# The diagonal of the other core's rows, masked through V instead of through the exponential

## The reference, cut to what matters

```python
s = einsum('bqhcd,bkhcd->bhcqk', qb, k) * scale          # two maps c per head h
s = where(dist >= 0, s - slope[h] * dist, -inf)          # causal, ALiBi
p = softmax(s)
a = p[:, :, 0] - lam * p[:, :, 1]
o = einsum('bhqk,bkhv->bqhv', a, v)                      # 4 heads, 128 value columns
```

## Time and profile before

| | us |
|---|---|
| median of 3 runs | 1221.82 (1221.73 to 1221.93) |
| the profiled execution, its own time | 1218.94 |
| its span on the slowest core (6) | 1217.4 |
| PE busy | 1154.6 (95%) |
| ACT busy | 652.8 (54%) |
| DVE busy | 601.8 (49%) |
| POOL busy | 80.7 (7%) |

### The profile page before, as it was taken

One profiled execution on the slowest core, in us unless ns is written; L12 is line 12 of the kernel. 1 busy time (PEld: TensorE's weight loads), 2 busy tenths in 40 slices (PEclk: granted clock), 3 DMA queues, 4 the chain that ended last, 5 costly groups with the idle time before them and its releaser, 6 DMA issues.

```text
span 1217.4 us, 27397 instructions; the slowest of 8 cores (1213.7 to 1217.4 us)
## 1 busy us (share of the span) xinstructions
PE 1154.6 (95%) x7340; PEld 578.0 (47%) x7464; DVE 601.8 (49%) x971; ACT 652.8 (54%) x1055; POOL 80.7 (7%) x139
## 2 busy tenths in 40 slices
PE   3799999999999999999999999999999999999995
PEld 1455444555555555554444444444444444444443
DVE  2666436553444333333365337336455463727767
ACT  4555358889898998976746773330211112030065
POOL 0000012111110000010000000000000000000012
PEclk9999999999999999999999999999999999999998
DMA  8487320002000000049441408011230403030124
GB/s 174 157 192 190 65 36 2 2 3 37 3 2 3 2 2 2 3 65 199 119 104 27 114 3 140 15 35 24 47 53 17 70 1 70 1 70 10 27 87 191
DMA packets 16903, 71.90 MB, mean 59 GB/s; under 512 B 2128, under 2 KB 2384, under 8 KB 14320
## 3 DMA queue, kind: packets, MB, share of 16 engines
q0 software_dynamic: 6768, 35.65, 17.9%
q1 hardware_dynamic: 9840, 33.97, 8.1%
q10 hardware_dynamic: 144, 0.52, 0.1%
HBM read 97.40 MB, written 8.39 MB: 87 GB/s over the span
## 4 chain that ended last, share of the span: by engine, by line
PE 88%; DMA 3%; DVE 3%; issue 3%; ACT 2%; DVEq 0%; SPq 0%; ACTq 0%; POOL 0%; POOLq 0%
PE ps_all L290 68%; PE ps_all L287 11%; PE ps_all L292 7%; DMA big<-w_g 2%; PE ps_all L311 2%; ACT big L582 1%; DVE big L314 1%; DMA big<-xs 1%; ACT big L298 0%; DVE big L1102 0%; DVE big L1120 0%; PE ps_all L657 0%; DVE big L625 0%; DVE big L974 0%; DVE big L1090 0%
## 5 line engine op out<-in xcount | busy, mean ns | idle before, releaser
L290 PE MATMUL ps_all<-big 128*128 128x512 bf16 (+2 forms) x4068 | 901.3, 375 | 27.2 <-DVE big L314 13.4
L290 PEld LDWEIGHTS ps_all<-big 128*128 128x128 bf16 x4192 | 394.3, 98 | 484.1 <-issue 43.1
L582 ACT ACTIVATE big<-ps_all,big 128x1024 bf16<-128x1024 f32 (+3 forms) x428 | 324.8, 802 | 38.2 <-PE ps_all L287 14.6
L1075 ACT ACTIVATE big<-ps_all 128x512 bf16<-128x512 f32 x124 | 74.1, 598 | 334.0 <-PE ps_all L290 333.8
L1102 DVE TENSOR_TENSOR big<-ps_all,big 128x512 f32<-128x512 f32 x256 | 176.6, 691 | 39.5 <-PE ps_all L290 36.1
L287 PE MATMUL ps_all<-big 128*128 128x129 bf16 x2176 | 163.6, 221 | 3.9 <-DVE big L625 1.8
L287 PEld LDWEIGHTS ps_all<-big 128*128 128x128 bf16 x2176 | 126.8, 98 | 54.5 <-issue 45.7
L1076 DVE TENSOR_TENSOR big<-big 128x512 bf16<-128x512 bf16 x124 | 53.0, 427 | 162.0 <-ACT big L1075 162.0
L292 PE MATMUL ps_all<-big 64*128 64x512 bf16 (+3 forms) x640 | 108.7, 352 | 3.6 <-ACT big L582 2.3
L298 ACT ACTIVATE big<-big 128x1024 bf16<-128x1024 f32 (+1 forms) x65 | 68.7, 1056 | 60.1 <-PE ps_all L290 25.2
L314 DVE TENSOR_TENSOR big<-ps_all,big 128x1024 bf16<-128x1024 bf16 (+1 forms) x49 | 58.9, 1205 | 40.7 <-PE ps_all L311 40.7
(11 more groups left out here) (60 smaller groups left out, 416.8 us busy)
## 6 DMA issues: line engine op xcount, KB each, us to landing
big<-xs SPq DMA_DIRECT2D x48, 512.0 KB, 6.5
big<-w POOLq DMA_DIRECT2D x16, 1024.0 KB, 12.8
big<-w_g POOLq DMA_DIRECT2D x16, 512.0 KB, 7.9
out<-big SPq DMA_DIRECT2D x15, 512.0 KB, 2.6
big<-w_in POOLq DMA_DIRECT2D x12, 512.0 KB, 8.0
big<-w_o POOLq DMA_DIRECT2D x1, 2048.0 KB, 24.4
big<-w_a POOLq DMA_DIRECT2D x1, 1024.0 KB, 10.9
big<-w_b POOLq DMA_DIRECT2D x1, 1024.0 KB, 11.0
```

What stands on the lines that cost most here:

```text
L290: S.op("pe", lambda e: e.matmul(out, lhsT, rhs, start=start, stop=stop), reads=reads, writes=writes)
L582: S.op("act", lambda e, a=a, b=b, bi=bi: e.activation(PT[:, :, a:b], Sps[:, buf, :, a:b], AF.Exp, bias=btab[:, bi:bi + 1], scale=0.125), r ...
L1075: S.op("act", lambda e: e.activation(r, ph, AF.Relu), reads=[phk], writes=[rk])
```

## The change

The own piece of the kind 1 diagonal goes for the tiles in `by_v`: c = 0, 1, 2 in heads 1 to 3, and c = 0, 2 in head 0. There the 128 columns are part of the neighbouring piece, without -30000. For those blocks PV takes a copy `Vm` of the tile's values and ones, times 0 (par 0) or 1 (par 1), instead of V. The factor comes as an input `keep` of 128 x 8, by core. `cut_v` makes the copies of a head's two or three tiles in one DVE multiplication; it is issued ahead of the stage for head 0 and, for each later head, ahead of the first PV of the head before. Two copies alternate. The planner adds 0.3 us to DVE's clock for each, and its estimates for exponentials follow the smaller number of pieces.

```diff
+    keep_d = din("keep", [128, 8])
+    keep = pers.take([128, 8], F32)
         if j == 20:
             ld("sp", btab, btab_d, "btab")
+            ld("sp", keep, keep_d, "keep")
             ld("sp", lamv, lam_d.partition_broadcast(128), "lamv")
+    Vm = ar.take([128, 2, 3, 130], BF16)
+    def by_v(h):
+        return (0, 1, 2) if h else (0, 2)
+
+    def cut_v(hid):
+        i, h = hid // 4, hid % 4
+        cs = by_v(h)
+        n, d = len(cs), cs[1] - cs[0]
+        k0 = 16 + 4 * i
+        src, dst = Vh[:, k0:k0 + d * (n - 1) + 1:d, h, 0:129], Vm[:, hid % 2, 0:d * (n - 1) + 1:d, 0:129]
+        S.op("dve", lambda e: e.tensor_scalar_mul(dst, src, keep[:, 0:1]),
+             reads=["V%d" % (k0 + c) for c in cs] + ["Vones", "keep"], writes=["Vm%d" % (hid % 2)])
     def exp_pieces(st):
-            if diag and kind == 1:
+            if diag and kind == 1 and cc % 4 not in by_v(st["h"]):
     def emit_pv(n):
-                    mm(Ops[:, g // 3, g % 3, :], PT[:, m, a:a + 128], Vh[:, kt, h, 0:129],
+                    vm = diag and kind == 1 and 128 * qc == cs and cc % 4 in by_v(h)
+                    mm(Ops[:, g // 3, g % 3, :], PT[:, m, a:a + 128],
+                       Vm[:, st["hid"] % 2, cc % 4, 0:129] if vm else Vh[:, kt, h, 0:129],
-                       reads=["V%d" % kt, "Vones", ptkey], writes=["pb%d" % (4 + g // 3)], shared=True)
+                       reads=["Vm%d" % (st["hid"] % 2) if vm else "V%d" % kt, "Vones", ptkey], writes=["pb%d" % (4 + g // 3)], shared=True)
+    cut_v(0)
     while pv_n < NS:
             st = steps[pv_n]
             set_mode(0)
+            if st["first"] and st["hid"] < 15:
+                cut_v(st["hid"] + 1)
+                clk["dve"] += 0.3
             emit_pv(pv_n)
+        m["keep"] = np.full((128, 8), 0.0 if par == 0 else 1.0, dtype=np.float32)
```

More of the change, by code:

```diff
@@ L504, in build_program @@
     WA_OFF = TOT - 8192
+    Vm = ar.take([128, 2, 3, 130], BF16)
     assert ar.p <= WA_OFF
     Wa = region(WA_OFF, 8192).take([128, 4, 1024], BF16)
-    at_keys = ["att0", "att1", "att2", "ato", "aton0", "aton1", "atrec", "atss", "atrs"] + hb_ring.keys + cg_ring.keys + acc_ring.keys
+    at_keys = ["att0", "att1", "att2", "ato", "aton0", "aton1", "atrec", "atss", "atrs", "Vm0", "Vm1"] + hb_ring.keys + cg_ring.keys + acc_ring.keys
     S.reuse(at_keys + ["Wa"], up_keys)
```

## The result

The changed kernel takes 1232.07 us (median of four runs, 1230.48 to 1233.97) where the kernel before takes 1221.88 beside it: a ratio of 1.0084, with a 95% interval of 1.0067 to 1.0101. It is 10.2 us slower; forecast were 3.0 us less. The time lies outside the range, on the other side. In some executions of any of these kernels one die has a lower granted clock and the time is longer; all times and ratios here leave those out.

A forecast was written before the change was run, and what follows sets the result against it. The prediction took PE to bound attention, ACT second by a small margin. Gains of 2.7 us in attention and 0.3 in the tail, copies and order at 0, gave 1221.82 - 3.0 = 1218.8 us; range 1215.3 to 1224.2.

The forecast's parts named there:

- The new waits are passed when they come: Attention stage: the copies' waits on V and earlier copies, and PE's on the copies, are already met; cost 0.
- (d): POOL queue: Wb's load lands ahead of a last-head causal select, its 18 us of waits delaying PV; 1233 us, chance 0.03.
- What bounds: Attention stage: PE is the bound by a small margin, busy 349.9 of 363.6 us; ACT is second at 324.8.
- (b): Attention stage: ACT paces more than PE's idle time shows, so 6 us are gained; 1215.8 us, chance 0.14.
- Pieces and their cost: Attention exponentials: 44 of 428 pieces go, 11.3 us of ACT busy time, 15.4 us counting waits between pieces.
- Worth 2.7 us in attention: PE in attention: 2.3 us of QK waits on ACT and 0.4 us of stalls inside PV groups go.
- (a): Attention: nothing is left of the gain, 3 us return as waits on DVE or Wb; 1221.8 us, chance 0.27.
- (c): Head turns in attention: PV waits for DVE's eviction instead of exponentials, five more such waits, 5.3 us; 1224.1 us, chance 0.10.
- Copies at 0: DVE in attention: sixteen copies, 6.6 us in all, lie beside PE's work and cost 0, at worst 6.6 us.
- What moves, 0 with 2.5 to either side: Planned attention order: the plan sees 12.3 us less ACT time, side matmuls move between tiles; 0, 2.5 us either way.
- the number of turns stays: Planned attention order: a QK still stands alone between other groups because of its two buffers; no added cost.
- Wb and POOL: Tail: Wb's load sits behind 17.96 us of some 450 POOL waits, 40 ns each; tail gain credited at 0.3 us.

The follow-up runs named there:

- the waits in another order: Changed kernel with SP's waits on DVE put behind its waits on PE, nothing else moved: 1221.3 us, ratio 0.9997 to the kernel before.
- the old order: Changed kernel, SP's DVE waits behind PE's, TensorE ordered as in the kernel before: 1217.87 us with copies; 1220.42 us without copies or zeroing.
- one wait per semaphore: Each instruction keeps only each semaphore's highest wait: kernel before 1217.06 us; changed kernel 1218.52; changed kernel with TensorE ordered as before 1214.74.
- the new order: TensorE's order as planned with the merged pieces' lower costs; changed kernel with SP's DVE waits behind PE's: 1221.3 us; without copies or zeroing: 1221.75.

## Why the prediction was wrong

The step that failed is "The new waits are passed when they come". It asked what the copies wait for, and that part holds: the copies' rows have 0.0 us of idle time before them. It did not ask who waits for the copies. A new reader of V adds a wait to whatever overwrites V, and that is the x loads on SP, 150 us later in the program. The text had seen the mechanism a few paragraphs earlier, on POOL ahead of Wb, and treated it as a bound for the gain; SP's queue with ten times as many waits had no term. Of the rivals only (d) was about a queue of waits, and it put them on the wrong engine. The term stood at 0; the runs show 9.8 us in its place (gates to MLP 230.2 us with the waits in another order, 240.0 without).

By its other steps:

- **What bounds:** right. PE was the bound; 11.3 us less ACT time moved attention by 1.6 us, and rival (b) did not come.
- **Pieces and their cost:** right, 44 fewer and 11.3 us.
- **Worth 2.7 us in attention:** the waits named went (2.4 to 0.6), but most of that came back at the evictions, as (a) and (c) described it; the prediction's own sign of (c), more than 3 us of waits there, is just met in the planned order (3.1). In the old order 0.9 us were left with the copies, 1.6 without them. With one wait per semaphore it is 2.0 (cores at full clock: 360.0 to 360.1 against 358.0): the term then is nearly right.
- **Copies at 0:** too low. In the old order about 0.7 us of attention, with 0.8 us more waiting for evictions (2.7 against 1.9 us); in the new order nothing. One profile of each; the cores agree within 0.2 us, the times do not settle it.
- **What moves, 0 with 2.5 to either side:** the mis-sized term. The order costs 1.7 us, and 1.4 more where the clock falls with it: 3.1, just outside, and enough to turn the forecast's gain into a loss of 1.5 us even with SP's queue mended and equal tails (1218.52 against 1217.06). That "the number of turns stays" did not protect it.
- **Wb and POOL:** the 17.96 us are the same to the hundredth, so it is indeed a count of waits; but they are 295, not some 450, and 0.061 us each, not 0.040.

Why the order is worse is shown only in part. PE's waits sum to 5.3 us in the new order on core 7 and to 3.7 in the old on core 3, which fits the 1.7 us of difference. Of these 1.6 us the evictions, seven places instead of five, are only 0.4; 0.9 are put down to DVE's reciprocal (L640), and 0.5 are QK's waits on ACT (0.2 fall away elsewhere). Which of the planner's moves makes them was not tried.

## What to carry to other kernels

Before pricing a cheap instruction, list the later instructions that must wait for it, on every engine and DMA queue, above all loads that reuse the memory it reads. A wait that has been met still costs its turn in the queue, so give an instruction one wait per semaphore; here that alone is worth about 3 us. And when a planner orders the work by cost estimates, price an edit once with the old order pinned, or the order's own effect is taken for the edit's.

## What was not expected of the hardware

SP passed waits that were met at 0.053 us each, POOL at 0.061. An idle stretch of 8.6 us cost PE another 2.8 us afterwards at the lower clock. A 0.28 us product on DVE took 2.26 us where one on POOL had begun 0.24 us ahead of it, on all eight cores of the programs that had the meeting, and 0.28 where it began 0.11 us ahead itself.
